# mLSTM queries and keys in six full tiles of 128 channels instead of eight of 96, in a two-layer block kernel

## What is computed

```python
mq, mk, mv, mo, mi, mf, ... = split_cols(h @ w_in[l], IN_SIZES)      # mq, mk: 384 channels each
qk = silu(causal_depthwise_conv(concat([mq, mk]), m_conv_w[l], m_conv_b[l]))   # width 4
mq, mk = qk[..., :384], qk[..., 384:]
# per head of 96 channels, chunks of 128 tokens; C, n, m: the state carried from chunk to chunk
s   = einsum('bhld,bhsd->bhls', qt, kt) * w_intra
num = einsum('bhls,bhsd->bhld', s, vt) + w_inter[..., None] * einsum('bhvk,bhlk->bhlv', C, qt)
den = sum(s, -1) + w_inter * einsum('bhk,bhlk->bhl', n, qt)
h   = num / maximum(abs(den), exp(-m_row))[..., None]
C_new = a * C + einsum('bhs,bhsv,bhsk->bhvk', wg, vt, kt)
n_new = a * n + einsum('bhs,bhsk->bhk', wg, kt)
```

## Time and profile before

| | |
|---|---|
| runs | 1096.48, 1093.76, 1094.71 us; median 1094.71 |
| the profiled execution | 1094.1 us |
| its span, first to last instruction | 1091.8 us |
| PE matmul busy | 1049.1 us, 96% |
| PE weight load busy (beside matmuls) | 537.1 us, 49% |
| DVE, ACT, POOL busy | 399.7, 280.4, 97.6 us |
| moved by DMA | 280.43 MB, mean 257 GB/s |
| mean granted TensorE clock | 0.997 |

### The profile page before, as it was taken

One profiled execution on the slowest core, in us unless ns is written; L12 is line 12 of the kernel. 1 busy time (PEld: TensorE's weight loads), 2 busy tenths in 40 slices (PEclk: granted clock), 3 DMA queues, 4 the chain that ended last, 5 costly groups with the idle time before them and its releaser, 6 DMA issues.

```text
span 1091.8 us, 12927 instructions
## 1 busy us (share of the span) xinstructions
PE 1049.1 (96%) x4575; PEld 537.1 (49%) x4609; DVE 399.7 (37%) x975; ACT 280.4 (26%) x536; POOL 97.6 (9%) x144
## 2 busy tenths in 40 slices
PE   6999999999999999999999999999999999999998
PEld 3577655333333334676654333333334844555543
DVE  1164425344444341462334444334430222333221
ACT  3244332111111103335332111111112005564300
POOL 1320211000000002210221000000000200000000
PEclk9999999999999999999999999999999999999999
DMA  8627228999999996328247999999979437822000
GB/s 295 202 78 258 103 85 296 385 412 412 410 413 413 412 391 215 104 79 308 78 155 279 395 412 412 413 412 411 413 295 389 184 37 211 308 79 77 1 1 38
DMA packets 95325, 280.43 MB, mean 257 GB/s; under 512 B 15957, under 2 KB 29699, under 8 KB 86960
## 3 DMA queue, kind: packets, MB, share of 16 engines
q1 hardware_dynamic: 90208, 273.27, 66.3%
q0 software_dynamic: 5072, 6.56, 1.8%
HBM read 286.98 MB, written 4.72 MB: 267 GB/s over the span
## 4 chain that ended last, share of the span: by engine, by line
PE 75%; SPq 13%; DMA 5%; ACT 3%; issue 2%; DVE 1%; ACTq 0%; DVEq 0%
PE bank L923 13%; PE bank L1472 13%; SPq L585 10%; PE bank L1035 8%; PE bank L955 7%; PE bank L1049 5%; PE bank L874 5%; PE bank L1232 5%; DMA ring<-in_w 3%; PE bank L1618 3%; PE bank L1602 3%; PE bank L1490 3%; SPq L591 2%; PE bank L863 2%; DMA ring<-in_w_in 2%
## 5 line engine op out<-in xcount | busy, mean ns | idle before, releaser
L923 PE MATMUL bank<-ring,arena 128*64 128x512 f32 x1024 | 229.2, 596 | 4.3 <-DMA ring<-in_w 4.2
L1472 PE MATMUL bank<-ring,xfT 128*128 128x512 f32 x320 | 141.5, 596 | 0.0
L923 PEld LDWEIGHTS bank<-ring,arena 128*64 128x64 f32 x1024 | 70.8, 137 | 136.6 <-issue 126.4
L955 PE MATMUL bank<-ring,arena 128*64 128x512 f32 x512 | 116.9, 599 | 0.0
L1035 PE MATMUL bank<-ring,xfT 128*128 128x384 f32 (+2 forms) x256 | 99.7, 542 | 4.5 <-DMA ring<-in_w_in 4.5
L1472 PEld LDWEIGHTS bank<-ring,xfT 128*128 128x128 f32 x320 | 59.3, 190 | 69.3 <-issue 68.3
L874 PE MATMUL bank<-arena 128*128 128x512 bf16 x352 | 86.4, 379 | 1.9 <-issue 0.3
L1640 ACT ACTIVATE arena<-bank 128x512 bf16<-128x512 f32 (+1 forms) x64 | 38.2, 597 | 190.1 <-PE bank L955 190.1
L1985 DVE TENSOR_TENSOR arena<-bank,arena 128x512 f32<-128x512 f32 x60 | 41.5, 691 | 119.4 <-ACT arena L1640 119.4
L1035 PEld LDWEIGHTS bank<-ring,xfT 128*128 128x128 f32 x256 | 49.2, 198 | 44.4 <-issue 25.5
L955 PEld LDWEIGHTS bank<-ring,arena 128*64 128x64 f32 x512 | 33.9, 136 | 68.4 <-issue 68.4
(11 more groups left out here) (381 smaller groups left out, 1128.7 us busy)
## 6 DMA issues: line engine op xcount, KB each, us to landing
ring<-in_w SPq DMA_DIRECT2D x256, 512.0 KB, 13.2
ring<-in_w SPq DMA_DIRECT2D x64, 1024.0 KB, 13.6
ring<-in_w_in SPq DMA_DIRECT2D x14, 2048.0 KB, 16.7
ring<-in_w_in SPq DMA_DIRECT2D x8, 1536.0 KB, 17.1
ring<-in_w_out SPq DMA_DIRECT2D x6, 2048.0 KB, 7.8
x_store<-x POOLq DMA_DIRECT2D x4, 512.0 KB, 6.1
ring<-in_w_up_moba SPq DMA_DIRECT2D x1, 2048.0 KB, 18.3
ring<-in_w_up_sb SPq DMA_DIRECT2D x1, 2048.0 KB, 8.7
```

Source lines behind the costliest of these rows:

```text
L923: ins = pe.matmul(bank[5][CELL * e:CELL * (e + 1), :], xg[:, par, 4 * h + k, at:at + CELL], view[:, e, :, k, :], start=(h == 0 and k == 0) ...
L955: ins = pe.matmul(bank[5 + n][CELL * e:CELL * (e + 1), :], turned[:, par, c, CELL * e:CELL * (e + 1)], down_view(s)[:, e, c, n * HALF:(n + ...
L1472: ins = pe.matmul(dst[:, :], xfT[:, k, t * P:(t + 1) * P], w[:, k, :], start=(k == 0), stop=(k == KD - 1))
```

## The change

The 384 channels of queries, and those of keys, are cut into three tiles of 128 channels in place of four of 96. A tile holds parts of two heads: tile 0 has head 0 and 32 channels of head 1, tile 1 has 64 of head 1 and 64 of head 2, tile 2 has 32 of head 2 and head 3. So there are six pieces (head, tile): `PIECES`, (0,0), (1,0), (1,1), (2,1), (2,2), (3,2).

- `head_unit` makes two tiles for `q01` and `k01`, and one tile for `q23` and `k23`. The convolution and the turning of the small weights run over six tiles in place of eight heads.
- The Silu of the queries becomes six activations of 256 tokens, one for each piece, with a scale on each partition from a new constant table `piece`, which is one inside the head and zero outside it. The result, `q_pieces`, is zero outside its head. The keys are not masked; their Silu is one activation over three tiles.
- `decay_scores` and `inter` take six matmuls for four heads, the two pieces of heads 1 and 2 being summed in PSUM. `state` has six products of 128 x 97 in place of four of 96 x 97; five lie in bank 4 and the sixth in a new use `state5` of bank 7, and each is copied out.

```diff
-                    for h in range(2):
+                    for c in range(2 * i, min(2 * i + 2, M_TILES)):
+                        at = c % 2 * SEQ
                         for k in range(KD):
-                            ins = pe.matmul(dst[hd, h * SEQ:(h + 1) * SEQ],
-                                            unit_view(u, M_WIDTH)[:, k, (2 * i + h) * M_DIM:(2 * i + h + 1) * M_DIM],
+                            ins = pe.matmul(dst[:, at:at + SEQ], unit_view(u, M_WIDTH)[:, k, c * P:(c + 1) * P],
                                             xfT[:, k, :], start=(k == 0), stop=(k == KD - 1))
...
                 def decay_scores(t):
                     dst = open_bank(f"st{t}")
-                    for h in range(M_HEADS):
-                        ins = pe.matmul(dst[:, h * P:(h + 1) * P], conv_out[hd, M_HEADS + h, t * P:(t + 1) * P],
-                                        conv_out[hd, h, t * P:(t + 1) * P], start=True, stop=True)
+                    for i, (h, c) in enumerate(PIECES):
+                        ins = pe.matmul(dst[:, h * P:(h + 1) * P], conv_out[:, M_TILES + c, t * P:(t + 1) * P],
+                                        q_pieces[i][:, t * P:(t + 1) * P], start=first_of(i), stop=last_of(i))
...
-                for h in range(M_HEADS):
-                    ins = pe.transpose(dst[:, h * M_DIM:(h + 1) * M_DIM], conv_out[hd, M_HEADS + h, 0:P],
-                                       ident[hd, 0:M_DIM])
+                for c in range(M_TILES):
+                    ins = pe.transpose(dst[:, c * P:(c + 1) * P], conv_out[:, M_TILES + c, 0:P], ident)
...
-                for h in range(M_HEADS):
-                    at = h * (M_DIM + 1)
-                    ins = pe.matmul(dst[hd, at:at + M_DIM + 1], k_weighted[:, h, :], proj_v[:, 0, h, :],
+                for i, (h, c) in enumerate(PIECES):
+                    if i == 5:
+                        done(ins, "state")
+                        dst = open_bank("state5")
+                    at = i % 5 * (M_DIM + 1)
+                    ins = pe.matmul(dst[:, at:at + M_DIM + 1], k_by_tile[:, c, :], proj_v[:, 0, h, :],
                                     start=True, stop=True)
-                done(ins, "state")
+                done(ins, "state5")
...
-                for h in range(M_HEADS):
+                for i, (h, c) in enumerate(PIECES):
                     at = h * (M_DIM + 1)
-                    ins = pe.matmul(dst[:, at:at + M_DIM + 1], conv_out[hd, h, P:SEQ], state[hd, h, :],
-                                    start=True, stop=True)
+                    ins = pe.matmul(dst[:, at:at + M_DIM + 1], q_pieces[i][:, P:SEQ], state[:, i, :],
+                                    start=first_of(i), stop=last_of(i))
...
-                part = conv_out[hd, 0:M_HEADS, :]
-                act.activation(part, part, ACT.Silu).then_inc(conv_act, 1)
+                for i, (h, c) in enumerate(PIECES):
+                    ins = act.activation(q_pieces[i], conv_out[:, c, :], ACT.Silu, scale=const["piece"][:, i:i + 1])
+                ins.then_inc(conv_act, 1)
...
-                copy_out("state", state[hd, :, :],
-                         lambda b: b[hd, 0:M_HEADS * (M_DIM + 1)].rearrange("p (h d) -> p h d", h=M_HEADS))
+                copy_out("state", state[:, 0:5, :],
+                         lambda b: b[:, 0:5 * (M_DIM + 1)].rearrange("p (i d) -> p i d", i=5))
+                copy_out("state5", state[:, 5, :], lambda b: b[:, 0:M_DIM + 1])
...
-                convolve("q23", 2, True)
+                convolve("q23", 2, 1, True)
...
-                convolve("k01", 4, False)
+                convolve("k01", 3, 2, False)
...
-                convolve("k23", 6, True)
+                convolve("k23", 5, 1, True)
```

More of the change, by code:

```diff
@@ L45 @@
 M_WIDTH = M_HEADS * M_DIM
+M_TILES = M_WIDTH // 128
+PIECES = [(h, c) for h in range(M_HEADS) for c in range(M_TILES)
+          if h * M_DIM < 128 * (c + 1) and 128 * c < (h + 1) * M_DIM]
 A_HEADS, NOPE, ROPE, V_DIM = 6, 64, 32, 64
@@ L149, in constant_table @@
         "row_limit": np.where(p == 0, SEQ - 1.0, NO_TOKEN),
+        "piece": np.concatenate([(p + P * c) // M_DIM == h for h, c in PIECES], axis=1),
     }
@@ L295, in program @@
         biased = nxt(NT, NE)
-        conv_raw = place(0, 2 * M_HEADS, 3 + SEQ)
+        conv_raw = place(0, 2 * M_TILES, 3 + SEQ)
         m_square = place(0, NT, M_WIDTH)
@@ L303, in program @@
         at[0] = 2 * M_HEADS * (3 + SEQ)
-        conv_out = nxt(2 * M_HEADS, SEQ)
+        conv_out = nxt(2 * M_TILES, SEQ)
+        q_pieces = [place(SEQ * i, SEQ) for i in range(3)] + [nxt(SEQ), nxt(SEQ), place(2 * M_HEADS * SEQ - SEQ, SEQ)]
         decay_at = at[0]
@@ L325, in program @@
         k_weighted = place(gelu_at, M_HEADS, M_DIM)
+        k_by_tile = place(gelu_at, M_TILES, P)
         ukv_at = at[0]
@@ L329, in program @@
         total = place(ukv_at, M_HEADS, M_DIM + 1)
-        state = place(ukv_at + M_HEADS * (M_DIM + 1), M_HEADS, M_DIM + 1)
+        state = place(ukv_at + M_HEADS * (M_DIM + 1), len(PIECES), M_DIM + 1)
         qkT_at = at[0]
@@ L1046, in head_unit @@
                     lands(u, 1)
[L1047 removed]
+                    for c in range(2 * i, min(2 * i + 2, M_TILES)):
+                        at = c % 2 * SEQ
                         for k in range(KD):
[L1049 to L1050 removed]
+                            ins = pe.matmul(dst[:, at:at + SEQ], unit_view(u, M_WIDTH)[:, k, c * P:(c + 1) * P],
                                             xfT[:, k, :], start=(k == 0), stop=(k == KD - 1))
[L1052 removed]
+                            if release is not None and c == 0 and k == 0:
                                 ins.then_inc(freed[release], 1)
@@ L1111, in mix @@
                 dst = open_bank("small")
-                for h in range(2 * M_HEADS):
-                    pe.transpose(dst[hd, 5 * h:5 * h + 5], conv_rows[0:5, h * M_DIM:(h + 1) * M_DIM], ident[0:5, 0:5])
+                for c in range(2 * M_TILES):
+                    pe.transpose(dst[:, 5 * c:5 * c + 5], conv_rows[0:5, c * P:(c + 1) * P], ident[0:5, 0:5])
                 pe.transpose(dst[:, 40:44], cb_rows[0:4, :], ident[0:4, 0:4])
@@ L1746, in mix @@
                 act.wait_ge(conv_ready, 2 * l + 2)
-                part = conv_out[hd, M_HEADS:, :]
+                part = conv_out[:, M_TILES:, :]
                 act.activation(part, part, ACT.Silu).then_inc(conv_act, 1)
@@ L2231, in mix, with heads, convolve @@
                 dve.nop().then_inc(left(plan, "rs"), 1)
[L2233 to L2237, removed]
+                def heads(name, first, n):
+                    src = full(dve, plan, name)[:, 0:n * SEQ].rearrange("p (c s) -> p c s", c=n)
+                    dve.tensor_tensor(conv_raw[:, first:first + n, 3:], src,
+                                      rstd_row.unsqueeze(1).broadcast_to([P, n, SEQ]), ALU.mult)\
                        .then_inc(left(plan, name), 1)
-                def convolve(names, first, signal):
-                    heads(names, first)
-                    for h in range(first, first + 2):
+                def convolve(names, first, n, signal):
+                    heads(names, first, n)
+                    for c in range(first, first + n):
                         copied(dve, plan, names)
-                        dst = conv_out[hd, h, :]
-                        step(dve.tensor_scalar(dst, conv_raw[hd, h, 3:3 + SEQ], conv_w[hd, h, 3:4],
-                                               conv_w[hd, h, 4:5], ALU.mult, ALU.add))
+                        dst = conv_out[:, c, :]
+                        step(dve.tensor_scalar(dst, conv_raw[:, c, 3:3 + SEQ], conv_w[:, c, 3:4],
+                                               conv_w[:, c, 4:5], ALU.mult, ALU.add))
                         for j in range(3):
-                            ins = dve.scalar_tensor_tensor(dst, conv_raw[hd, h, j:j + SEQ], conv_w[hd, h, j:j + 1],
+                            ins = dve.scalar_tensor_tensor(dst, conv_raw[:, c, j:j + SEQ], conv_w[:, c, j:j + 1],
                                                            dst, ALU.mult, ALU.add)
-                            if j < 2 or not signal or h == first:
+                            if j < 2 or not signal or c < first + n - 1:
                                 step(ins)
```

16 lines of the change are left out of this document (10 added, 6 removed), and 1 row of the table MIXER_BANKS.

## The result

| | before | after |
|---|---|---|
| median | 1095.0 us (1093.76 to 1096.48, 4 runs) | 1082.53 us (1080.66 to 1084.96, 4 runs) |
| ratio | | 0.9887, interval 0.9865 to 0.9909 |
| profiled execution, its span | 1094.1, 1091.8 us | 1084.96, 1082.7 us |

The change is faster by 12.5 us, about 1.1%. Forecast were 1083 us and a range of 1080.0 to 1088.1. A second measurement, further down, gives 0.9877 (0.9858 to 0.9897).

A forecast was written before the change was run, and what follows sets the result against it. PE, busy 96% of the span, was taken as the bound; -6.91 + 0.89 + 0.34 + 0.10 = -5.58 us a layer, -11.2 for two, took 1094.1 to 1083 us, range 1080.0 to 1088.1.

The forecast's parts named there:

- The projections: Query and key projections on PE: 48 matmuls in place of 64 at the same price, 6.91 us less a layer.
- The first rival: Projections: loads of 128 weight columns not hidden, 27 ns more each, 2.6 us a layer, result 1088.1; chance 5%.
- The added work: Extra mixer work a layer: decay scores +0.89 us, the state +0.34, inter +0.10.
- Decay scores: Four more matmuls of 0.222 us on PE, covered by no wait: +0.89 us a layer.
- The state: Six products for four; ACT's longer and extra copies delay PE before attend_values(3): +0.34 us a layer.
- inter: Six matmuls for four, +0.43 us on PE; a 0.33 us wait for ACT goes, +0.10 us stays.
- DVE and ACT hidden: Convolutions and Silu in the mixer: both engines' changed work stays hidden behind PE; ACT's uncovered price 1.1 us.
- A margin of 10.9 us becomes 9.8: From the keys' Silu on ACT to PE's need of the keys: slack shrinks but keeps the work hidden.
- Through the expert stage: Expert stages, both layers: weight loads are released by PE, so the pattern moves with PE and its length stays.
- The second rival: Expert stage: the weight stream starts at its own time and holds the end; 1094.1 us, no change; chance 4%.
- The clock: Attention part: longer PE waits drop the clock to 1.2 GHz, 7.3 us a layer lost, 1097.4 or more; chance 3%.
- The sum: Whole kernel: -5.58 us a layer, -11.2 us for two, from 1094.1 to 1083 us.

The follow-up runs named there:

- a_redo: The changed kernel with the single tile of the second query and key groups projected twice, so 64 matmuls a layer again; 1095.86 us, ratio 1.0005.
- b_wide: The old kernel with 128 columns of weights in place of 96 in its 64 query and key matmuls a layer; 1094.28 us, ratio 0.9993.
- a_late_state: The changed kernel with ACT's copies of the state moved behind its copy of head 3's turned probabilities; 1082.28 us, ratio 0.9889.
- b_three: The old kernel without the projection of head 3 of queries and keys, DVE and ACT work as before; 1087.15 us, ratio 0.9922.
- a_half_k: The changed kernel with queries and keys projected from the first half of the model width, 24 matmuls a layer; one execution of 1064.78 us.
- a_conv_twice: The changed kernel with four more convolutions of a key tile on DVE in each layer; 1099.19 us, ratio 1.0037.
- b_again: The old kernel once more, unedited, for a second profile; one execution of 1094.41 us.

## Why the prediction was right

**The projections: -6.91 us a layer.** Right to the digit. `a_redo` gives exactly 6.91 back in each layer, and `b_wide` shows that width is nearly free: the loads grew from 163 to 190 ns, and the mixer by 0.08 us. The first rival had its own test in `b_wide` and would have shown 6.9 us.

**The added work: +1.33 us forecast, 1.18 measured** (`a_redo`). Decay scores 0.90 (forecast 0.89). The state 3.19 - 2.95 = 0.24 (0.34): PE's wait was 0.51 us where I had reckoned 0.64, because three copies in a row cost ACT 1.09 us, 0.24 more than the two before, and not 0.34. `inter` 4.11 - 4.12 = -0.01 (0.10). The rest, about 0.06, lies ahead of the decay scores, where the sum had nothing; `b_wide`'s 0.08 for the width is of that size, and the turned keys take as long as before. The mechanisms were the ones named: `a_late_state` took the copies away from ahead of the wait, and the wait with them.

**DVE and ACT hidden: right, but for a wrong reason, and nearly not.** The step that failed is "A margin of 10.9 us becomes 9.8". I took the margin from the Silu's end to PE's decay scores. But ACT works in order, and behind the keys' Silu stand the gates and the turned heads. PE waits for the last of these, 1.6 us before it comes to the decay scores, and for 1.22 us in both kernels (PE's timeline, before and after):

```profile
100.84 0.32 PE L1174 MATMUL bank<-masks_bf,ident_bf 128*128 128x384 bf16 x1 [1.22 <-ACT arena L1757]
...
94.30 0.32 PE L1181 MATMUL bank<-masks_bf,ident_bf 128*128 128x384 bf16 x1 [1.22 <-ACT arena L1773]
```

The slack that counts is ACT's idle time in that row. In the old kernel it was 2.48 us:

```profile
98.34 0.58 ACT L1752 ACTIVATE arena<-bank,stats 128x384 f32<-128x384 f32 x1 [2.48 <-PE bank L1035]
```

In the changed one it is 1.47. So the loss of 1.1 us that I had worked out was right, 1.0 measured; the margin that it was taken from was not 10.9 but 2.5. The runs show it from three sides: 2.0 us more on DVE cost 0.44 us, 8.0 cost 6.48, and where only PE's work was taken away (`b_three`) 0.9 of 6.91 us went back. So, going by `b_three`, the two tiles that DVE no longer convolves are worth 0.9 us a layer, where I had put their worth at nothing. That the sum came out well with a margin of 9.8 in it is luck: 2 us more on DVE, which 9.8 would have hidden, cost time.

**Through the expert stage.** Right: 233.45 and 234.65 us after, 234.08 and 234.25 before; the second profiles have 233.94 and 234.13 after, 234.06 and 234.26 before. `a_half_k` started the stages 16 and 33 us earlier than the old kernel, and they grew by 1 us. The second rival falls with that: the stream starts when PE frees buffers and moves with it. Layer 0's pairs show it again, in SP's timeline of the changed kernel against the earlier trace rows:

```profile
305.91 11.13 SPq L592 DMA_DIRECT2D ring<-in_w  x8
...
321.53 12.32 SPq L592 DMA_DIRECT2D ring<-in_w  x8
```

The pair that came at 311.29 comes 5.38 us earlier, and the next one 6.04.

**The clock.** The rival asked for a fall in the mixers of the changed kernel; its windows of 20 us from 40 to 160 us all have 1.00, and so have those from 442 to 563. But it is no idle fear: behind a wait of 7.7 us (`a_conv_twice`) and, in one layer of two, behind one of 2.1 (`b_three`) the clock fell, for 1.6 to 1.9 us a layer beyond the wait, and in layer 0 of `b_wide` and `b_again` it fell near 165 us, for 0.8 and 0.7 us. None of these comes near the 7.3 us a layer that the rival needed.

**The sum.** The experts of layer 0 start 5.4 us earlier and those of layer 1 12.7; forecast were 5.6 and 11.2; the 1.5 us beyond are the start, the way and layer 0's expert stage of the ledger, which vary by as much between profiles of one kernel. -11.2 forecast, -11.46 in the mixers, -12.5 and -12.3 by medians. The first interval, -14.8 to -10.0, holds all of these, the second, -15.5 to -11.3, all but the forecast, by 0.1 us. The 1 us between stages and medians is at the edge of what the runs can tell, and its cause is not shown.

## What to carry to other kernels

With float32 matmuls that stream 256 columns, PE paid for the number of matmuls, not for how much of the array each fills: cut the other dimension into full tiles of 128, and let zeros in the smaller operand keep the heads apart. With 97 columns streamed it was not so: the state's products took 0.17 us each with 96 columns of weights and 0.22 with 128 (1.32 us for six). Price what comes in with it from rows of the same form, and read slack from the idle time of every in-order engine between the producer and the one that waits, not from the distance of two events. Where executions differ by several us, compare the length of a stage from one named instruction to another; here a mixer repeats to 0.04 us at the full clock and decides what five rounds of times can't.

## What the hardware showed that I had not expected

The granted clock over the same work with the same two short waits (1.42 and 0.99 us) was 1.00 in one execution and 0.74 in another, and the difference is 1.9 us of 27.7 at this place, 2.65 with the turns ahead. The same happened behind a wait in layer 1 of `b_three` (0.91) and not in its layer 0. So with PE nearly always busy, a short wait leaves the full clock in some executions and not in others; the falls found here cost from 0.7 us (`b_again`, layer 0) to 2.65.

How much of the spread of the runs (1080.4 to 1085.8 us for the changed kernel) is that? Each execution's mean granted clock is on record. Of 45 executions of the old kernel, the 15 with 0.994 and less took 1095.7 us in the mean, the 14 with 0.997 and more 1093.6: so a part. But two of the changed kernel, both with 0.995, took 1080.66 and 1084.96 us. The profiles show where the rest can lie: in the start (42.7 to 48.4 us) and in the way between the layers (38.0 to 41.9), of which the first holds waits for DMA and the second the gaps of 0.6 us and more that no releaser explains.
